# Branch projections moved into the waves of a recurrence, and two out products begun inside attention

## The reference, cut to what matters

```python
# first block, each layer l
x = x + 0.5 * swiglu(norm(x))
x = x + concat(attention_heads(norm(x))) @ w_out[l]
x = x + 0.5 * swiglu(norm(x))
# second block
gates  = sigmoid(u[..., RW_COLS + MLA_COLS:])              # 2 x 1024 columns
y_rw   = rwkv7_time_mix(...)     # scan in two directions, group norm, bonus, output gate; 512 wide
y_mla  = mla_mix(...)            # 8 heads of softmax attention; 512 wide
merged = gates[:, :, 0] * (y_rw @ w_br_rwkv) + gates[:, :, 1] * (y_mla @ w_br_mla)
x = x + merged @ w_out_2
x = x + peer_ffn(...); x = x + side(...); return rmsnorm(x)
```

## Time and profile before

| | us |
|---|---|
| median of 3 runs | 2289.1 |
| lowest and highest run | 2287.02, 2296.77 |
| the profiled execution, its own time | 2297.99 |
| its span | 2296.2 |
| PE busy in it | 2030.1 (88%) |
| DVE, ACT, POOL busy | 1274.1, 805.8, 655.2 |
| mean granted TensorE clock | 0.955 |

### The profile page before, as it was taken

One profiled execution on the slowest core, in us unless ns is written; L12 is line 12 of the kernel. 1 busy time (PEld: TensorE's weight loads), 2 busy tenths in 40 slices (PEclk: granted clock), 3 DMA queues, 4 the chain that ended last, 5 costly groups with the idle time before them and its releaser, 6 DMA issues.

```text
span 2296.2 us, 35217 instructions
## 1 busy us (share of the span) xinstructions
PE 2030.1 (88%) x14096; PEld 1641.8 (72%) x14096; DVE 1274.1 (55%) x2330; ACT 805.8 (35%) x1336; POOL 655.2 (29%) x671
## 2 busy tenths in 40 slices
PE   7999989999999999999988999986778677668867
PEld 7999969999999988999877887872333333224425
DVE  5555635655564664654565443285666566666543
ACT  5434335444443454433663323121211222112222
POOL 0000010000000100000002322047777777777772
PEclk9999989999999999999999998998899988989998
DMA  9553506554654524654305000579999999999993
GB/s 307 195 182 118 184 1 220 181 185 146 203 172 157 174 66 136 195 188 128 126 1 178 26 21 27 181 261 369 360 397 372 361 364 367 357 369 368 363 378 145
DMA packets 254878, 489.60 MB, mean 213 GB/s; under 512 B 13936, under 2 KB 174224, under 8 KB 254624
## 3 DMA queue, kind: packets, MB, share of 16 engines
q0 software_dynamic: 73888, 268.53, 31.1%
q1 hardware_dynamic: 177104, 214.32, 28.8%
q10 hardware_dynamic: 3760, 5.02, 0.7%
HBM read 486.74 MB, written 1.05 MB: 212 GB/s over the span
## 4 chain that ended last, share of the span: by engine, by line
PE 66%; POOL 14%; DMA 6%; issue 6%; DVE 5%; ACT 3%; POOLq 0%; DVEq 0%; ACTq 0%
PE bank L763 65%; POOL arena_sb L2720 11%; POOL con_sb L2720 3%; DMA arena_sb<-peer_u,arena_sb 2%; DMA con_sb<-peer_v,arena_sb 2%; DMA arena_sb<-peer_v,arena_sb 1%; DVE parts_sb L2033 0%; PE bank L914 0%; DVE xT_sb L2097 0%; DVE parts_sb L2028 0%; DVE sq_sb L2592 0%; DVE arena_sb L2439 0%; ACT parts_sb L1558 0%; DMA xT_sb<-xT 0%; DMA ring_sb<-ffn_w_gate 0%
## 5 line engine op out<-in xcount | busy, mean ns | idle before, releaser
L763 PE MATMUL bank<-arena_sb 64*64 64x64 f32 (+7 forms) x3688 | 516.3, 324 | 156.1 <-ACT arena_sb L1984 112.6
L763 PE MATMUL bank<-xh_sb,parts_sb 128*128 128x256 f32 x3328 | 605.2, 284 | 19.6 <-DVE parts_sb L2028 16.2
L763 PEld LDWEIGHTS bank<-arena_sb 64*64 64x64 f32 (+4 forms) x3688 | 301.7, 162 | 362.2 <-issue 219.4
L763 PEld LDWEIGHTS bank<-xh_sb,parts_sb 128*128 128x128 f32 x3328 | 514.5, 190 | 25.9 <-issue 25.0
L763 PE MATMUL bank<-xl_sb,parts_sb 128*128 128x256 f32 x1808 | 509.7, 282 | 0.0
L2592 DVE CUSTOM_DVE_ANT_0 sq_sb<-arena_sb 128x1024 f32<-128x1024 f32 x256 | 309.6, 1224 | 265.8 <-DMA arena_sb<-peer_u,arena_sb 262.8
L2028 DVE TENSOR_TENSOR parts_sb<-ring_sb,parts_sb 128x2048 fp32r<-128x2048 f32 x132 | 298.7, 2290 | 174.6 <-ACT parts_sb L1544 174.6
L763 PEld LDWEIGHTS bank<-xl_sb,parts_sb 128*128 128x128 f32 x1808 | 343.5, 190 | 0.0
L2720 POOL DMA_INDIRECT arena_sb<-peer_u,arena_sb x256 | 278.0, 1086 | 196.8 <-DVE arena_sb L2540 113.0
L1544 ACT ACTIVATE parts_sb<-ring_sb 128x2048 fp32r<-128x2048 f32 x132 | 248.0, 1909 | 59.6 <-PE bank L763 58.3
L763 PE MATMUL bank<-h_high_sb,parts_sb 128*128 128x256 f32 x1408 | 255.8, 282 | 0.0
(11 more groups left out here) (273 smaller groups left out, 1871.2 us busy)
## 6 DMA issues: line engine op xcount, KB each, us to landing
ring_sb<-ffn_w_gate SPq DMA_DIRECT2D x44, 1024.0 KB, 5.4
ring_sb<-ffn_w_up SPq DMA_DIRECT2D x44, 1024.0 KB, 6.7
ring_sb<-ffn_w_down SPq DMA_DIRECT2D x44, 1024.0 KB, 5.0
ring_sb<-w_in SPq DMA_DIRECT2D x17, 1024.0 KB, 6.0
ring_sb<-w_in_ab SPq DMA_DIRECT2D x12, 1024.0 KB, 5.2
ring_sb<-w_out SPq DMA_DIRECT2D x12, 1024.0 KB, 5.2
ring_sb<-w_in_cd SPq DMA_DIRECT2D x12, 1024.0 KB, 5.3
ring_sb<-peer_w_q SPq DMA_DIRECT2D x8, 1024.0 KB, 5.3
```

The lines of the kernel that those rows point to most:

```text
L763: return pe.matmul(dst, lhsT, rhs, start=start, stop=stop_, skip_group_check=loose)
```

## The change

Of the eight units of the latent branch, five are moved into the waves: units 0, 1 and 2 stand in the first three waves between TT of level 5 and W of level 6, unit 3 there in the fourth wave, and unit 4 in the fourth wave between TT of level 6 and U. All use bank 3, and ACT copies them (to `MTW`, in space that the value chunks held) in the same places of its own order. Units 5, 6, 7 stand behind the group variances, in banks 5, 6, 7. DVE multiplies the two parts by their gates in two instructions. The slot of the first latent branch weights is fetched ahead of the last gate slot.

In layers 0 and 1 of the first block the output chunks m = 4 to 7 (banks 2 and 3) are begun inside the last attention steps: in layer 0 with kk = 0 at t = 4, kk = 4, 1 at t = 5, and kk = 5, 2 at t = 6; in layer 1 with kk = 4, 5 at t = 9, kk = 6, 7 at t = 10 and kk = 0, 1 at t = 11. Each stands ahead of that step's `soft_mixed`. The out product then does m = 0 to 3 in full and adds only the missing kk to m = 4 to 7. The third out product has no early part.

```diff
-        at["gates"] = k; k += 8
-        at["br"] = k; k += 4
+        for s in range(7):
+            at["gates", s] = k; k += 1
+        at["br", 0] = k; k += 1
+        at["gates", 7] = k; k += 1
+        for s in range(1, 4):
+            at["br", s] = k; k += 1
...
+        WAVE_BRANCH = [(0,), (1,), (2,), (3, 4)]
+        MTW = view(2048, 5, T)
...
+                    for m in WAVE_BRANCH[w][l - 5 : l - 4] if l >= 5 else ():
+                        plan(("br", 1, m), 3)
...
-        for m in range(8):
+        for m in (5, 6, 7):
             plan(("br", 1, m), 4 + m % 4)
...
+            OUT_EARLY = {0: ((0,), (4, 1), (5, 2)), 1: ((4, 5), (6, 7), (0, 1)), 2: ()}
+            def out_early(l, i):
+                for kk in OUT_EARLY[l][i]:
+                    out_ready(l, kk)
+                    for m in range(4, 8):
+                        k = at["wo", l] + m // 2
+                        first = kk == OUT_EARLY[l][0][0]
+                        if first and m % 2 == 0:
+                            have(k)
+                            fill_begin(pe, ("y", l, m // 2))
+                        b = bank[fill_of["y", l, m // 2][0]]
+                        ins = mm(b[:, (m % 2) * T : (m % 2 + 1) * T], ..., MIX[:, kk, :], first and m % 2 == 0, False, loose=True)
...
+                    if early and m >= 4:
+                        rest = [kk for kk in order if kk not in early]
+                        for kk in rest:
+                            ins = mm(..., src[:, kk, :], False, kk == rest[-1], loose=True)
...
+                    if l == 1 and t >= 9:
+                        out_early(1, t - 9)
                     if t >= 4:
                         soft_mixed(l, t - 4)
...
+                    if t >= 4:
+                        out_early(0, t - 4)
                     if t >= 3:
                         soft_mixed(0, t - 3)
...                                           # PE, wave w, after TT of level l
+                        for m in WAVE_BRANCH[w][l - 5 : l - 4] if l >= 5 else ():
+                            branch_part(1, m)
...                                           # PE, behind the waves
+                for m in (5, 6, 7):
+                    branch_part(1, m)
+                pe.wait_ge(S("y_rw_ready"), 2)
+                for m in range(8):
+                    branch_part(0, m)
+                out_product(2, MG)
...                                           # ACT, wave w, after its W copies of level l
+                        for m in WAVE_BRANCH[w][l - 5 : l - 4] if l >= 5 else ():
+                            branch_out(m)
...                                           # DVE
-                for m in range(4, 8):
+                emptied(dve, ("br", 1, 4))
+                link(dve.tensor_tensor(MTW, MTW, GATES[:, 8:13, :], ALU.mult))
+                for m in (5, 6, 7):
                     emptied(dve, ("br", 1, m))
-                link(dve.tensor_tensor(MT, MT, GATES[:, 8:16, :], ALU.mult))
+                link(dve.tensor_tensor(MT[:, 5:8, :], MT[:, 5:8, :], GATES[:, 13:16, :], ALU.mult))
```

More of the change, by code:

```diff
@@ L733, in _, with gate_weights, branch_weights @@
                 in2(i)
-            for s in range(8):
-                k = at["gates"] + s
+            def gate_weights(s):
+                k = at["gates", s]
                 fetch(k, slot(k, KC, 256), rows(w2)[:, :, 2336 + 256 * s : 2592 + 256 * s])
[L737 to L740, removed]
+            def branch_weights(s):
+                k, w = at["br", s], (A["w_br_mla_2"][0], A["w_br_rwkv_2"][0])[s // 2]
+                fetch(k, slot(k, 4, 512), rows(w)[:, :, s % 2 * 512 : (s % 2 + 1) * 512])
+            for s in range(7):
+                gate_weights(s)
+            branch_weights(0)
+            gate_weights(7)
+            for s in range(1, 4):
+                branch_weights(s)
             square(at["wo", 2], A["w_out_2"][0], 4)
@@ L854, in ffn, with out_ready, out_product @@
                 down(CHUNKS - 1, 0)
-            def out_product(l, n_wait, src, order=range(KC)):
-                for m in range(KC):
+            OUT_EARLY = {0: ((0,), (4, 1), (5, 2)), 1: ((4, 5), (6, 7), (0, 1)), 2: ()}
+            def out_ready(l, kk):
+                if l == 0:
+                    emptied(pe, ("o", 0, kk) if kk < 4 else ("mt", 0, kk - 4))
+                elif l == 1:
+                    emptied(pe, ("mt", 1, (kk + 4) % 8))
+                else:
+                    pe.wait_ge(S("merged"), kk + 1)
+            def out_early(l, i):
[8 more added lines that the diff above has]
+                        b = bank[fill_of["y", l, m // 2][0]]
+                        ins = mm(b[:, (m % 2) * T : (m % 2 + 1) * T], slot(k, KC, 256)[:, kk, (m % 2) * P : (m % 2 + 1) * P],
+                                 MIX[:, kk, :], first and m % 2 == 0, False, loose=True)
+                        if first and m == 4:
+                            release(ins)
+            def out_product(l, src, order=range(KC)):
+                early = [kk for kks in OUT_EARLY[l] for kk in kks]
+                for m in range(KC):
+                    if early and m >= 4:
+                        k, b = at["wo", l] + m // 2, bank[fill_of["y", l, m // 2][0]]
+                        rest = [kk for kk in order if kk not in early]
+                        for kk in rest:
+                            ins = mm(b[:, (m % 2) * T : (m % 2 + 1) * T], slot(k, KC, 256)[:, kk, (m % 2) * P : (m % 2 + 1) * P],
+                                     src[:, kk, :], False, kk == rest[-1], loose=True)
+                            if kk == rest[0]:
+                                release(ins)
+                        if m % 2:
+                            fill_end(ins, ("y", l, m // 2))
+                            owed[0] += 1
+                        continue
                     k = at["wo", l] + m // 2
@@ L864, in out_product @@
                         if m == 0:
-                            n_wait(kk)
+                            out_ready(l, kk)
                         ins = mm(b[:, (m % 2) * T : (m % 2 + 1) * T], slot(k, KC, 256)[:, kk, (m % 2) * P : (m % 2 + 1) * P],
@@ L1077, in layer @@
                     stick_and_soft()
-                    out_product(l, lambda kk: emptied(pe, ("o", 0, kk) if kk < 4 else ("mt", 0, kk - 4)), MIX)
+                    out_product(l, MIX)
                 else:
                     soft(1, 8)
-                    out_product(l, lambda kk: emptied(pe, ("mt", 1, (kk + 4) % 8)), MIX, PAIRS[1])
+                    out_product(l, MIX, PAIRS[1])
             def second_in():
@@ L1129, in gate @@
             def gate(m):
-                k = at["gates"] + m // 2
+                k = at["gates", m // 2]
                 if m % 2 == 0:
@@ L1233, in latent, with branch_part @@
                 soft(2, 4)
+            def branch_part(branch, m):
+                src = YM if branch else YR
+                k = at["br", 2 * (1 - branch) + m // 4]
+                b = fill_begin(pe, ("br", branch, m))
+                if m % 4 == 0:
+                    have(k)
+                for kk in range(4):
+                    ins = mm(b[:, 0:T], slot(k, 4, 512)[:, kk, (m % 4) * P : (m % 4 + 1) * P], src[:, kk, :], kk == 0, kk == 3)
+                    if kk == 0:
+                        release(ins)
+                fill_end(ins, ("br", branch, m))
+                if m % 4 == 3:
+                    owed[0] += 1
             def recurrence():
@@ L1250, in recurrence @@
                              ("bonus", j))
+                for pair in range(4):
+                    emptied(pe, ("mt", 2, pair))
                 for w, (d, c) in enumerate(WAVES):
@@ L1843, in latent, with branch_out @@
                 soft(2, 4, {1: key_roots, 4: lambda: factors(0), 5: lambda: factors(1)})
+            def branch_out(m):
+                b = take(act, ("br", 1, m))
+                give(act.activation(MTW[:, m, :] if m < 5 else MT[:, m, :], b[:, 0:T], ACT.Copy), ("br", 1, m))
             def recurrence():
@@ L1902, in recurrence @@
                 act.activation(GATES, GATES, ACT.Sigmoid).then_inc(S("gates_ready"), 1)
-                for m in range(8):
-                    b = take(act, ("br", 1, m))
-                    give(act.activation(MT[:, m, :], b[:, 0:T], ACT.Copy), ("br", 1, m))
+                for m in (5, 6, 7):
+                    branch_out(m)
                 act.dma_start(PIN, rows(A["pT"])).then_inc(S("p_loaded"), 16)
@@ L2484, in branches_out @@
                     emptied(dve, ("br", 0, m))
-                    dve.tensor_tensor(MG[:, m, :], MG[:, m, :], MT[:, m, :], ALU.add).then_inc(S("merged"), 1)
+                    dve.tensor_tensor(MG[:, m, :], MG[:, m, :], (MTW if m < 5 else MT)[:, m, :], ALU.add).then_inc(S("merged"), 1)
                 residual(("y", 2))
```

## The result

| | before | after |
|---|---|---|
| median of 7 runs, us | 2289.16 | 2272.76 |
| lowest and highest | 2282.86, 2301.05 | 2265.47, 2284.59 |
| profiled execution, its span | 2296.2 | 2282.9 |
| mean granted clock | 0.955 | 0.958 |

The ratio of the times is 0.9917, 95% interval 0.9894 to 0.9941: 19 us faster, between 14 and 24. The forecast was 10.3 us (2278.8). Either way the gain is above the 8 to 13 us that the sum allowed, and beyond the bound of 11.4 us, which the prediction gave 0.37.

The account below looks back on a forecast made before the run. PE at the matmul helper was 65% of the span; only idle and half-clock time could be won. 6.5 + 1.35 - 0.2 + 3.7 = 11.3 us, cut to 10.3 for a median run: 2289.1 - 10.3 = 2278.8, range 2271 to 2287.

Parts of the forecast that it names:

- the bound of 11.4 us: Whole kernel: 0.5% of its time, under which its runs can't be told from no change; faster given 0.37.
- Layer 0's stretch: Layer 0, end of step 4's values to the out product's end: about 31.8 us, before 38.3, at clock 1.00.
- Layer 1's idle time: Layer 1, PE gaps before step 10's values and before the last pair, covered by early matmuls: 1.35 us won.
- rival 1: Layer 0: the clock falls all the same, leaving 7.5 us won in all, 2281.6; chance 0.16.
- The bank wait: Behind the waves: PE's 2.29 us wait for bank 4 goes, and 1.9 us waiting for DVE's `YR` appears.
- rival 4: Feed-forwards: late-released w_out slots starve them; 14.5 us cost against 10.3 won at a 17 us fetch, 2293.3; chance 0.05.
- A unit before level 6: Each of the four waves: the branch unit there makes U start 0.9 us later, bounds 0.4 and 2.5.
- rival 2: Waves: units cost their full 2.5 us each; 2285.2, halfway 2282; chance 0.12.
- Together the waves get 5.3 us longer: Four waves: 3.6 us for units ahead of level 6 plus 1.7 us for unit 4 ahead of U.
- Rival 3: Fourth wave: unit 4 keeps the clock up, 3.7 us more won, 14.0 in all, 2275; chance 0.18.
- layer 0's half-clock term: Layer 0: 3.9 us won if the clock stays up, about 2.9 of it counted for a median run.
- what the early parts push back: Layers 0 and 1: later slot releases and last banks closer together, charged 0.1 us a layer.

Follow-up runs that it names:

- extra_in_waves: Old kernel with five added units in the waves whose result nobody reads, the real units left behind the norm; ratio to the old kernel 1.0000 (0.9973 to 1.0026).
- branch_only: Changed kernel without the early parts of the out products, only the branch units moved; ratio to the old kernel 0.9969 (0.9951 to 0.9987).
- unit4_behind: Changed kernel with unit 4 moved from the fourth wave to behind the group norm; ratios to the old kernel 0.9926 and, run again, 0.9916.

## Why the prediction was wrong

**Right.** Layer 0's stretch, idle time and clock together: 31.3 us for 31.8 forecast. Layer 1's idle time: 1.6 us for 1.35. The clock of layer 0 stays up, and rival 1, which would have kept it falling, did not come true with one 0.52 us gap left. By the section of the Trainium skill that the prediction names ("TensorE: Matmul & The Clock Gate", "A second HAM failure mode: psum-queue depth-cycling") such a gap could have been enough; in the eight profiles with the early part it was not. The bank wait turned into the wait for `YR`, 1.90 us. No feed-forward starved: rival 4 is out. A unit before level 6 cost 0.9 to 1.3 us for 0.9; rival 2's 2.5 us did not come.

The terms of the forecast, beside what the profiles give for the same stretches (us gained; from the end of step 4's values to the first gather):

| stretch | forecast | first pair of profiles | mean of three and three |
|---|---|---|---|
| to the end of layer 0's product | 5.5 | 7.0 | 7.1 |
| to the end of layer 1's product | 1.35 | 1.6 | 1.8 |
| to the first Gram products | -0.2 | -1.8 | -1.6 |
| the waves | -5.3 | -6.1 | -1.5 |
| from the group norm to the first gather | 9.0 | 8.7 | 8.0 |
| sum | 10.3 | 9.4 | 13.8 |

**The step that failed** is "Together the waves get 5.3 us longer". As a delay at a given clock it is even too small: 0.99, 0.87, 0.99 and 1.34 us in the four waves and 2.1 for unit 4, 6.3 us by the spans of the first profile, and that first pair, 173.6 and 179.7 us, seems to bear it out. As a change of the stage it is wrong: -1.5 us between the three profiles of each kernel, and 0 on average over all twelve with no or five units, as the units halve the time at 1.2 GHz. The half clock goes ahead of the place that the units left, and `extra_in_waves`, with nothing removed, ties with the old kernel. The term thus took the old trace's clock as given. In its own size, 5.3 us against 0 to 1.5, this is most of the 6 to 9 us missed.

Rival 3, at 0.18, named the mechanism, but for the fourth wave, and there it did not come in the changed kernel: from DVE's level-6 copies to the last O read are 14.3 us in its first profile, 12.5 before, about unit 4's price more, and its other two profiles have half clock there too. It did come in `branch_only` and in the first profile of `unit4_behind`, so it varies. What it held against itself, that "U and O themselves are as sparse as before", was true as well. The mechanism should have been asked of the first three waves, where most of the half clock went.

**The base was one profile.** It had 21 us at half clock in the waves where the six other profiles without units have 32 to 40. From it the clock's share in the waves looked small, and the pair of profiles showed 9.65 us ahead of the gather. Counted from the end of step 4's values to the first gather, the three profiles of each kernel give 1184, 1192, 1195 before and 1175, 1178, 1177 after: 13.8 us on average.

**Smaller errors.** I cut layer 0's half-clock term for the median, from 3.9 to 2.9 us, on the guess that it comes and goes. It doesn't: all six profiles without the early part there have the stretch from 327 to 339, none of the eight with it. And I charged 0.2 us for what the early parts push back; the half clock behind the last norm costs 1.8. The last is a slip: 13 + 3.7 us below 2289.1 is 2272.4, where the range says 2271.

**Left open.** 13.8 us are ahead of the gather, and the three timed gains are 16 to 19. The stage behind it is 3.6, 2.4 and 4.4 us shorter in the changed kernel when the profiles are paired in order (the second pair from two sets), which would close the account, but kernels that differ only ahead of it spread over 10 us there (796.2 to 806.4 us in the first two sets of runs), so that it belongs to the change isn't shown.

## What to carry to other kernels

Where the granted clock falls in a stage of small matmuls with waits, independent dense matmuls put there can cost nothing even when the timeline shows no gap for them: here 8.6 us of them went with 18 us less at half clock. Price such a move with the clock, not at the clock of the old trace. Take a second profile before a sum rests on half-clock stretches; see which of them return. A stretch that returned in every profile (layer 0) can be counted in full.

## What the runs showed of the hardware that was not expected

PE was given 8.6 us more work in `extra_in_waves` and the kernel's time did not change (ratio 1.0000, 0.9973 to 1.0026), with the mean clock of the waves at 0.94, where six of the seven profiles without units have 0.89 to 0.91 and the seventh 0.94. And the same 2.6 us of idle time, after which the old kernel ran on at full clock (16 records in 3.61 us), was followed by half clock (5.08 to 5.30 us) when it came 2 to 9 us earlier, in all nine profiles of kernels with an early part and in none of the five others.
